# Second attention of a three-layer transformer kernel: scores from stacked parts, packed values, transfers on SyncE's queue

## The chip, the cores and the metric

The kernel runs as one program on one core of a Trainium2 chip. The metric is the device time of one execution in microseconds; lower is better. TensorE multiplies, VectorE (DVE) and ScalarE (ACT) work element by element, GpSimd (POOL) makes the low parts of weights, SyncE (SP) issues transfers.

## The reference, cut to what matters

A block of two layers is followed by a third of another kind, on 512 positions of width 1024. Layer 0 has differential attention, layer 1 (the "second attention" here) windowed attention with grouped keys, layer 2 forgetting attention beside a convolution. All arithmetic is float32. The second attention, cut down:

```
q, k, v = split(h @ w_qkv)           # 16 query heads, 4 key/value heads, head dim 64
q, k = rope(q), rope(k)
s = einsum(q, k) * 64**-0.5          # only |i-j| <= 128: blocks of 128, at most 3 key blocks
m = max(max(s), sink)                # one sink logit per head
e = exp(s - m)
pr = e / (sum(e) + exp(sink - m))
o = einsum(pr, v) @ w_o
```

h is the RMS-normed residual; the result is added to the residual.

## The kernel before, in words

**Float32 by two parts.** Each operand is split into a high part (dtype fp32r, the rounded value) and a low part (value minus high part). `mm3` makes a product of three matmuls: high x high, high x low, low x high. The product low x low is left out. ScalarE makes high parts, VectorE low parts; for weights GpSimd makes the low part.

**Weights.** They come as slabs of 128 x 1024 (512 KB). SyncE's `load` issues one transfer per slab, in order, into one of two raw buffers (`RAWS = 2`); load s waits until GpSimd has made the low part of slab s-2 (`lo_ready`). ScalarE's `high` makes the high part into a ring of four (`RING = 4`) when TensorE is done with the slab four earlier (`used`, `replaced`). All that is a fixed order on each engine: nothing overtakes. SyncE's queue holds the slab loads of the whole kernel and, in the first attention, small `exchange` transfers between partitions.

**The second attention** (kind 2). Stage `kq2a` has two slabs: the first pair of key heads and the first pair of query heads (tile j holds two heads). `v2` has two slabs for the values, and `kq2` eight slabs: the second pair of key heads, then the query tiles 1 to 7. After a tile is projected, ScalarE's `swap_halves` (L1187) makes four copies of 32x512 out of PSUM, VectorE's `rope` (L1716, L1717, L1720) rotates, `q_high` (ScalarE, L1193) and `q_low` (VectorE, L1743) make the parts in `qkhi`, `qklo`, indexed [partition, buffer, query or key, position]; a pair of heads takes partitions 0-63 and 64-127. TensorE's `project_qk` can do a part of a tile; `open_tile` waits until the PSUM bank is free, which `rope`'s first product releases (L1716). All tiles of `kq2` but the first use one bank, that of the last value tile too, which `values_low` (L1693) releases.

The values are written with zeros beside them (`padded`): the head u of a pair has its 64 columns at 64u of a 128-column block, high parts in `Bhi[1]`, low parts in `Blo[1]`. `zero_padding("v2")` clears the rest with four memsets. So both heads of a pair add into one PSUM tile of 128 rows (bank 7).

**Steps.** There are 8 pairs of heads j and 4 query blocks qb, in all 32 steps g = 4j + qb, and in each two heads s. In step g TensorE issues: `scores(g + 2)`, a quarter of a projection (`piece` says which; with g % 4 == 0 it comes last, `late`), `transposes(g)`, and in even steps `outputs(g - 1)`, for two query blocks. Projections end with step 23. `scores` (L708) makes for each of two heads an `mm3` on 64 partitions (columns: 256 or 384 keys), then masks by a product with the identity, once with the high constants and once with their copy in the other half of the partitions: ten matmuls a step, three of products and two of masks for each head. `outputs` (L777) makes 18 matmuls: 3 spans of keys x 2 heads x 3.

VectorE per step: `maxima(g + 2)` (L1753 to L1768), `rope` or `q_low` where a tile is due, `normalise(g + 1)` (L1782 to L1797), `prob_low(g)` (L1805). ScalarE per step: `exps(g + 1)` (L1207, L1216), `prob_high(g)` (L1228), `q_high`, every fourth step `evacuate` (L1235, a copy of 128x512 of bank 7 into `OA`), `swap_halves`, `replaced`. In the last steps `output_high` and `output_low` split `OA` for the output projection `o2`.

**Start.** TensorE: both tiles of `kq2a`, the values, `scores(2, 0)`, tile 0 of `kq2` (second keys), tile 1, `scores(2, 1)`, then the steps. ScalarE's order there: swaps, high parts of slabs 0 and 1 of `kq2`, `q_high`, high parts of slabs 2 and 3 of `kq2` (after the value slabs are used), then the high parts of the values.

## Time and profile before

| | us |
|---|---|
| median of 3 runs | 2091.57 |
| lowest, highest | 2088.61, 2092.48 |
| span of the profiled execution | 2087.8 |

The page gives no time of the profiled execution beyond its span. The span lies 3.8 us under the median of the runs. In it TensorE is busy 2043.2 us, VectorE 1224.2, ScalarE 941.6, GpSimd 904.8. The second attention's steps run from about 741 to 888 us.

How to read the rows. A timeline has the start in us, the length in us, the engine, the line in the kernel, the operation, out<-in by the program's names, the shapes and a count; in brackets the idle time before and what ended it. PE is TensorE's matmul, PEld its weight load, SPq SyncE's queue. Matmul ends are modelled, so rates are taken from start to start. A group adds the busy time (overlaps counted once) and the mean ns of one. In a table of stretches each engine has its busy us and its instructions; then come the granted clock of TensorE (1.00 is full), the busy share of the 16 DMA engines and the GB/s moved. A waits row says who waited for whom, us in total, times, the longest.

### The profile page before, as it was taken

How to read it: one execution, taken by the hardware profiler on the slowest of the kernel's cores; microseconds unless marked ns; L12 is line 12 of the kernel's file. 1: busy time of each engine (PE TensorE's matmuls, PEld its weight loads, DVE VectorE, ACT ScalarE, POOL GpSimd, SP SyncE). 2: the span in 40 equal slices, each digit the busy share in tenths (PEclk: the TensorE clock that was granted, in tenths of full speed). 3: DMA queues.
4: the chain of work that ended last, by engine and by line, in shares of the span. 5: the costliest groups of instructions: out<-in, count | busy, mean ns of one | idle time of the engine just before them, and what ended most of it. 6: DMA issues, size and time to landing. Idle time of an engine off the chain costs nothing.

```text
span 2087.8 us, 28730 instructions
## 1 busy us (share of the span) xinstructions
PE 2043.2 (98%) x9976; PEld 1684.1 (81%) x9976; DVE 1224.2 (59%) x1842; ACT 941.6 (45%) x1495; POOL 904.8 (43%) x660
## 2 busy tenths in 40 slices
PE   7999999999999999899999999999999999999999
PEld 6777788888887878788888887878888788888887
DVE  6677857546265789856636266548879473213222
ACT  5456645434245567635424245535742544322222
POOL 4322235545456431044645456444215454455454
PEclk9999999999999999999999999999999999999999
DMA  4222122332323211022333223222103222232323
GB/s 169 81 76 76 48 75 98 103 101 91 101 91 121 81 61 32 31 91 81 101 101 101 92 99 112 91 81 92 39 23 107 85 91 92 90 110 92 101 91 111
DMA packets 52756, 183.21 MB, mean 88 GB/s; under 512 B 6576, under 2 KB 6832, under 8 KB 52656
## 3 DMA queue, kind: packets, MB, share of 16 engines
q1 hardware_dynamic: 51072, 177.76, 25.9%
q10 hardware_dynamic: 1584, 4.07, 0.5%
q8 instruction: 68, 1.11, 0.2%
q14 instruction: 32, 0.26, 0.0%
HBM read 176.04 MB, written 2.10 MB: 85 GB/s over the span
## 4 chain that ended last, share of the span: by engine, by line
PE 53%; issue 24%; POOL 13%; DVE 7%; ACT 2%; POOLq 0%; DVEq 0%; DMA 0%; ACTq 0%; SPq 0%
PE PS L544 52%; POOL wlo L536 13%; DVE AR L1915 1%; PE PS L773 1%; DVE AR L1918 0%; DVE acc L1630 0%; DVE ptlo L1805 0%; DVE AR L1797 0%; DVE nmax L1753 0%; ACT AR L1187 0%; DVE AR L2277 0%; ACT AR L1323 0%; DVE AR L1931 0%; DVE Blo L1935 0%; DVE Blo L2281 0%
## 5 line engine op out<-in xcount | busy, mean ns | idle before, releaser
L536 POOL TENSOR_TENSOR wlo<-raw,whi 128x512 fp32r<-128x512 f32 x656 | 904.6, 1402 | 1169.7 <-ACT whi L1090 1168.5
L544 PE MATMUL PS<-Bhi,whi 128*128 128x512 f32 x2352 | 927.7, 394 | 17.2 <-DVE Blo L1623 10.8
L544 PE MATMUL PS<-Blo,whi 128*128 128x512 f32 x2352 | 917.6, 390 | 0.0
L544 PE MATMUL PS<-Bhi,wlo 128*128 128x512 f32 x2352 | 917.4, 390 | 0.0
L1090 ACT ACTIVATE whi<-raw 128x1024 fp32r<-128x1024 f32 x328 | 345.2, 1056 | 510.7 <-PE PS L544 435.4
L544 PEld LDWEIGHTS PS<-Bhi,whi 128*128 128x128 f32 x2352 | 442.5, 188 | 123.1 <-issue 14.1
L544 PEld LDWEIGHTS PS<-Bhi,wlo 128*128 128x128 f32 x2352 | 442.6, 188 | 93.7
L544 PEld LDWEIGHTS PS<-Blo,whi 128*128 128x128 f32 x2352 | 443.0, 188 | 89.3 <-issue 0.5
L1614 DVE TENSOR_TENSOR AR<-PS,R 128x512 f32<-128x512 f32 x170 | 115.3, 690 | 235.9 <-PE PS L544 224.1
L1670 DVE TENSOR_TENSOR X<-X,PS 128x512 f32<-128x512 f32 x88 | 60.3, 687 | 227.2 <-PE PS L544 226.5
L1915 DVE SCALAR_TENSOR_TENSOR AR<-AR,par_sb 128x511 f32<-128x511 f32 x88 | 117.6, 1336 | 8.8 <-ACT AR L1323 8.8
L1338 ACT ACTIVATE Bhi<-AR 128x512 f32 x66 | 41.8, 633 | 167.7 <-DVE AR L1931 167.7
L1918 DVE SCALAR_TENSOR_TENSOR AR<-AR,par_sb 128x511 f32<-128x511 f32 x88 | 106.8, 1213 | 12.9 <-DVE AR L1915 2.9
L1207 ACT ACTIVATE AR<-PS,nmax 128x512 f32<-128x512 f32 (+3 forms) x160 | 93.2, 590 | 44.1 <-DVE nmax L1756 41.7
L1323 ACT ACTIVATE AR<-AR,par_sb 128x512 f32<-128x512 f32 x88 | 71.0, 806 | 38.5 <-DVE AR L1614 38.5
L1935 DVE TENSOR_TENSOR Blo<-AR,Bhi 128x512 f32 x66 | 47.1, 714 | 62.1 <-ACT Bhi L1338 62.1
L1623 DVE SCALAR_TENSOR_TENSOR Blo<-X,par_sb,Bhi 128x512 fp32r<-128x512 f32 x56 | 63.0, 1135 | 34.9 <-ACT Bhi L1116 27.7
L1228 ACT ACTIVATE pthi<-PS 128x512 fp32r<-128x512 f32 (+3 forms) x128 | 56.4, 477 | 59.1 <-PE PS L773 58.4
L1931 DVE TENSOR_TENSOR AR<-AR 128x512 f32<-128x512 f32 x66 | 56.1, 849 | 36.3 <-ACT AR L1334 27.2
L1630 DVE TENSOR_TENSOR acc<-acc,sq 128x512 f32<-128x512 f32 x56 | 73.2, 1308 | 0.0
L773 PE MATMUL PS<-constR,AR 128*128 128x128 f32 x368 | 58.3, 286 | 10.6 <-DVE ptlo L1805 9.7
L1805 DVE TENSOR_TENSOR ptlo<-PS,pthi 128x512 fp32r<-128x512 f32 (+3 forms) x128 | 64.3, 534 | 6.7 <-ACT pthi L1228 6.7
(237 smaller groups left out, 2069.1 us busy)
## 6 DMA issues: line engine op xcount, KB each, us to landing
raw<-in_weights SPq DMA_DIRECT2D x328, 512.0 KB, 3.2
AR<-AR SPq DMA_DIRECT2D x56, 64.0 KB, 2.0
X<-in_xT ACTq DMA_DIRECT2D x4, 512.0 KB, 6.9
out<-X SPq DMA_DIRECT2D x8, 256.0 KB, 3.0
AR<-in_pT ACTq DMA_DIRECT2D x2, 512.0 KB, 3.9
par_sb<-in_parameters ACTq DMA_DIRECT2D x1, 314.0 KB, 8.5
AR<-in_positions ACTq DMA_DIRECT2D x1, 256.0 KB, 8.3
con_sb<-in_constants ACTq DMA_DIRECT2D x1, 198.5 KB, 8.1
```

The costliest lines, as they stand in the source:

```text
L536: ins = pool.tensor_tensor(wlo[:, j, c], raw[:, j % RAWS, c], f32(whi[:, j, c]), ALU.subtract)
L544: return pe.matmul(out, w, x, start=start, stop=stop)
L773: last = pe.transpose(PS[:, 2 + n % 2, k * P:k * P + P], source[:, k * P:k * P + P], ident)
L1090: act.activation(whi[:, slot, :], raw[:, slot % RAWS, :], ACT.Copy)\
L1207: act.activation(probs(kind)[:, 2 * (g % 2) + s, 0:nb * P], PS[:, score_bank(kind, n), 0:nb * P], ACT.Exp, bias=nmax[:, n % 4:n % 4 + 1], ...
L1323: act.activation(cv[:, 2 * pair + u, :], us[:, 2 * pair + u, :], ACT.Identity, scale=conv_w[:, l, 1, u, bass.ds(q, 1)], bias=conv_w[:, l, ...
L1614: tt(out, PS[:, bank, :], R[:, :], ALU.mult).then_inc(tile_free[bank], 1)
L1623: stt(chunks(Blo[b])[:, m, :], X[:, m, :], gain(name, col, m), f32(chunks(Bhi[b])[:, m, :]), ALU.mult, ALU.subtract).then_inc(x_split, 1)
L1630: tt(acc[:, :], acc[:, :], sq[:, slot, :], ALU.add).then_inc(sq_used, 1)
L1805: tt(transposed(ptlo, kind, g, s), PS[:, 2 + n % 2, 0:blocks * P] .rearrange("p (k q) -> p k q", k=blocks), f32(transposed(pthi, kind, g, s)),
L1915: own.step(stt(c[:, 1:T], x[:, 0:T - 1], conv_w[:, l, 0, u, bass.ds(q, 1)], c[:, 1:T], ALU.mult, ALU.add))
L1918: stt(c[:, 0:T - 1], x[:, 1:T], conv_w[:, l, 2, u, bass.ds(q, 1)], c[:, 0:T - 1], ALU.mult, ALU.add).then_inc(conv_done, 1)
```

## The change

Scores: `qkhi` and `qklo` become two halves of one tile `qk`. SyncE gets two new jobs. `stack_keys(kb)` makes four transfers of 256 KB that write the high and the low key parts of each head of pair kb into both halves of the partitions (`stackk`, in `Blo[1]`). `stack_queries(j)` makes four transfers of 128 KB that put a head's high query part into one half of the partitions and its low part into the other (`stackq`, in the end of `Bhi[1]`, two buffers). They wait for `q_ready`, and stand in SyncE's order ahead of the loads `of_k + 6`, `of_q + 6` and `of_q + j + 6`. With `of_q = of_k + 4`, the first keys and queries stand ahead of the load of slab 2 of `kq2`. TensorE's scores wait for the transfers and make per head two matmuls of 128 rows (the product low x low comes with them) and one mask.

Values: `padded(..., low=True)` writes the low part of a head into the other 64 columns of its block in `Bhi[1]`. `outputs` then makes two matmuls per span and head, 12 in all, and the two heads go to two halves of bank 7; the part from the low values lies in the other half of the partitions. `evacuate_part` (ScalarE, two copies of 64x256 across the halves) and `add_parts` (VectorE, two additions of 64x256) follow every second step; `outputs` waits for the last `add_parts`. `zero_padding("v2")` is gone.

Projections: `piece` is one step further on in kind 2 (a tile ends with g % 4 == 2), `late` is g % 4 == 3, and at g == 0 two quarters are made at the end of the step.

```diff
@@ -200,8 +200,8 @@
         Bhi = [sb(f"Bhi{n}", [P, KC * T], F32R) for n in range(2)]
         Blo = [sb(f"Blo{n}", [P, KC * T], F32R) for n in range(2)]
-        qkhi = sb("qkhi", [P, 2, 2, T], F32R)
-        qklo = sb("qklo", [P, 2, 2, T], F32R)
+        qk = sb("qk", [P, 2, 2, 2, T], F32R)
+        qkhi, qklo = qk[:, 0], qk[:, 1]
         pthi = sb("pthi", [P, 6, T], F32R)
         ptlo = sb("ptlo", [P, 6, T], F32R)
         R = sb("R", [P, T])
@@ -290,6 +290,11 @@
         cvo = ar(7296, 4)
         frow = AR[0:8, 3072:3072 + 3 * T].rearrange("p (n t) -> p n t", n=3)
         angs = ar(5120, 6)
+        stackq = Bhi[1][:, TB * T:].rearrange("p (b s t) -> p b s t", b=2, s=2)
+        stackk = Blo[1][:, :].rearrange("p (h l t) -> p h l t", h=4, l=2)
         raw_ready = [sem(f"raw_ready{n}") for n in range(RAWS)]
...
@@ -362,7 +370,7 @@
         PAIRS = {1: 8, 2: 8, 3: 4}
-        def padded(stage, B, src, t):
+        def padded(stage, B, src, t, low=False):
@@ -370,7 +378,8 @@
             v = B[1][:, 0:TB * nh * P].rearrange("p (k n c) -> p k n c", k=TB, n=nh)[:, t]
             v = v.rearrange("p (n two) c -> p n two c", two=2)
             s = src.rearrange("p (n two c) -> p n two c", two=2, c=64)
-            return [(v[:, :, u, 64 * u:64 * u + 64], s[:, :, u, :]) for u in range(2)]
+            at = [64 * u if not low else 64 - 64 * u for u in range(2)]
+            return [(v[:, :, u, at[u]:at[u] + 64], s[:, :, u, :]) for u in range(2)]
         def band(kind, qb):
@@ -388,7 +397,7 @@
         PB0 = {1: 0, 2: 32, 3: 96}
         GROUP = 2
         PV0 = {1: 0, 2: 16, 3: 32}
-        OP0 = {1: 0, 2: 8, 3: 16}
+        OP0 = {1: 0, 2: 8, 3: 24}
         QT0 = {1: 0, 2: 16, 3: 26}
@@ -398,7 +407,7 @@
-            first = 7 if kind == 1 else 8
+            first = {1: 7, 2: 9, 3: 8}[kind]
             p, r = (g + first) // 4, (g + first) % 4
             t, part, parts = {1: (2 * p - 2 + r // 2, r % 2, 2), 2: (p, r, 4),
                               3: (2 * p + r // 2, r % 2, 2)}[kind]
@@ -515,7 +524,45 @@
                 if first <= s < first + NPROJ[1]:
                     exchange(s - first + 2)
                 load(s, s % RAWS, s - 1)
-            with sp.Fori((first + NPROJ[1] + 3) // 4, SLABS // 4) as i:
+            def stack_keys(kb):
+                n = QT0[2] + 2 * kb
+                sp.wait_ge(q_ready, n + 1)
+                for s in range(2):
+                    rows = slice(64 * s, 64 * s + 64)
+                    for to in range(0, P, 64):
+                        sp.dma_start(f32(stackk[to:to + 64, 2 * kb + s, :, :]), f32(qk[rows, :, kb, 1, :]))\
+                            .then_inc(kstacked[kb], 16)
+            def stack_queries(j):
+                b = j % 2
+                sp.wait_ge(q_ready, QT0[2] + (1 if j == 0 else j + 2) + 1)
+                if j >= 2:
+                    sp.wait_ge(score_done, SC0[2] + 8 * (j - 1))
+                for s in range(2):
+                    rows = slice(64 * s, 64 * s + 64)
+                    for half in range(2):
+                        to = 64 * (half ^ s)
+                        sp.dma_start(f32(stackq[to:to + 64, b, s, :]), f32(qk[rows, half, b, 0, :]))\
+                            .then_inc(qstacked[b], 16)
+            begin, of_k, of_q = SLAB0["kq2a"] // 4 * 4, SLAB0["kq2a"], SLAB0["kq2"]
+            end = -(-(of_q + NPROJ[2] + 6) // 4) * 4
+            stacks = {of_k + 6: ((stack_keys, 0), (stack_queries, 0)), of_q + 6: ((stack_keys, 1),)}
+            for j in range(1, 8):
+                stacks[of_q + j + 6] = ((stack_queries, j),)
+            with sp.Fori((first + NPROJ[1] + 3) // 4, begin // 4) as i:
+                for j in range(4):
+                    load(4 * i + j, j % RAWS, 4 * i + j - 1)
+            for s in range(begin, end):
+                for stack, n in stacks.get(s, ()):
+                    stack(n)
+                load(s, s % RAWS, s - 1)
+            with sp.Fori(end // 4, SLABS // 4) as i:
                 for j in range(4):
                     load(4 * i + j, j % RAWS, 4 * i + j - 1)
             for m in range(KC):
@@ -710,14 +757,17 @@
                 b = j % 2
                 kb = j // 4 if kind == 2 else b
                 first, nb, masks = band(kind, qb)
-                if g == 0 and kind > 1:
+                if g == 0 and kind == 3:
                     pe.wait_ge(swapped_ready, 2)
                 if g == {2: 1, 3: 0}.get(kind):
                     all_values(kind)
-                if qb == 0:
-                    pe.wait_ge(q_ready, QT0[kind] + {1: 2 * j + 2, 2: 2 if j == 0 else j + 3,
-                                                     3: 2 * j + 2}[kind])
+                if qb == 0 and kind == 2:
+                    pe.wait_ge(qstacked[b], 64 * (j // 2 + 1))
+                    if j % 4 == 0:
+                        pe.wait_ge(kstacked[kb], 64)
+                elif qb == 0:
+                    pe.wait_ge(q_ready, QT0[kind] + 2 * j + 2)
                     if kind == 3 and j == 0:
                         pe.wait_ge(cc_ready, 1)
@@ -735,12 +785,21 @@
                     rows, cols = slice(64 * s, 64 * s + 64), slice(qb * P, qb * P + P)
                     keys = slice(first * P, (first + nb) * P)
                     out = PS[:, score_bank(kind, n), 0:nb * P]
+                    if kind == 2:
+                        for half in range(2):
+                            mm(out, stackq[:, b, s, cols], stackk[:, 2 * kb + s, half, keys],
+                               half == 0, False)
+                        blocks = out.rearrange("p (b c) -> p b c", c=P)
+                        at, c = [block for block, _ in masks], masks[0][1]
+                        mm(blocks[:, at[0]:at[-1] + 1:2, :], constR[:, 0, :], constR[:, c:c + len(masks), :],
+                           False, True).then_inc(score_done, 1)
+                        continue
                     last = mm3(out, qkhi[rows, b, 0, cols], qklo[rows, b, 0, cols],
                                qkhi[rows, kb, 1, keys], qklo[rows, kb, 1, keys], True, kind == 1)
                     if kind == 1:
                         last.then_inc(score_done, 1)
                     outs.append(out)
-                if kind == 1:
+                if kind < 3:
                     return
                 for s, out in enumerate(outs):
                     rows = slice(64 * s, 64 * s + 64)
@@ -780,7 +839,10 @@
                 heads = HP[kind]
                 pe.wait_ge(pt_ready, PB0[kind] + heads * (g + 1))
-                if last_qb == GROUP - 1 and OP0[kind] + j:
+                if kind == 2:
+                    pe.wait_ge(o_ready, OP0[2] + g // GROUP)
+                elif last_qb == GROUP - 1 and OP0[kind] + j:
                     pe.wait_ge(o_ready, OP0[kind] + j)
                 nh = {1: 8, 2: 4, 3: 8}[kind]
@@ -794,6 +856,18 @@
                     if qs:
                         spans.append((len(qs) == 2, k, qs[0], qs[-1] + 1))
                 spans.sort(reverse=True)
+                if kind == 2:
+                    for s in range(2):
+                        head = 2 * (j // 4) + s
+                        for n, (_, k, a, b) in enumerate(spans):
+                            r, c = row_of(kind, g, s, k), (a - q0) * P
+                            out = PS[:, 7, 2 * P * s + c:2 * P * s + (b - q0) * P]
+                            for half, buf in enumerate((pthi, ptlo)):
+                                last = mm(out, vhi[:, k, head, :], keys_of(buf, kind, g)[:, r, c:c + (b - a) * P],
+                                          n == 0 and half == 0, n == len(spans) - 1 and half == 1)
+                    last.then_inc(pv_done, 1)
+                    return
                 work = [(k, a, b, 0) for _, k, a, b in spans]
                 if kind != 1:
@@ -865,7 +939,7 @@
                 for g in range(steps):
                     if g + AHEAD[kind] < steps:
                         scores(kind, g + AHEAD[kind])
-                    late = kind == 2 and g % 4 == 0
+                    late = kind == 2 and (g % 4 == 3 or g == 0)
                     if piece(kind, g) and not late:
                         t, part, parts = piece(kind, g)
                         project_qk(PROJ[kind], norm, t - 2 if kind == 3 else t, part, parts)
@@ -889,6 +963,8 @@
                         half_tile("o1a", 0, range(4))
                     if piece(kind, g) and late:
                         t, part, parts = piece(kind, g)
+                        if g == 0:
+                            project_qk(PROJ[kind], norm, t, 0, parts)
                         project_qk(PROJ[kind], norm, t, part, parts)
                     if kind == 1 and g in SPREAD:
                         spread_factor(SPREAD[g])
...
@@ -1234,6 +1310,14 @@
                 act.wait_ge(pv_done, PV0[kind] + (j + 1) * (4 // GROUP))
                 act.activation((OA3 if kind == 3 else OA)[:, j, :], PS[:, 7, :], ACT.Copy)\
                    .then_inc(o_ready, 1)
+            def evacuate_part(e):
+                act.wait_ge(pv_done, PV0[2] + e + 1)
+                j, c = e // 2, slice(2 * P * (e % 2), 2 * P * (e % 2) + 2 * P)
+                act.activation(OA[0:64, j, c], PS[64:128, 7, 0:2 * P], ACT.Copy)
+                act.activation(OA[64:128, j, c], PS[0:64, 7, 2 * P:4 * P], ACT.Copy).then_inc(part_ready, 1)
             def output_square(h):
@@ -1275,7 +1359,9 @@
                         for c in OSPLIT.get(g, ()):
                             output_high(OA, c)
-                    if g % 4 == 0 and g:
+                    if kind == 2 and g % GROUP == 0 and g:
+                        evacuate_part(g // GROUP - 1)
+                    if kind != 2 and g % 4 == 0 and g:
                         evacuate(kind, g // 4 - 1)
                         if kind == 1:
                             output_square(g // 4 - 1)
...
@@ -1685,7 +1774,7 @@
                                  for b in (Blo[1], Bhi[1])]
                             parts = [(v[0], PS[:, bank, :], v[1])]
                         else:
-                            lo = padded(stage, Blo, PS[:, bank, 0:width], t)
+                            lo = padded(stage, Bhi if stage == "v2" else Blo, PS[:, bank, 0:width], t, stage == "v2")
                             hi = padded(stage, Bhi, PS[:, bank, 0:width], t)
                             parts = [(a, s, b) for (a, s), (b, _) in zip(lo, hi)]
                         for q, (out, src, hi) in enumerate(parts):
@@ -1838,10 +1927,21 @@
                 bank, _ = tile_of(stage, 0, m)
                 tt(X[:, m, :], X[:, m, :], PS[:, bank, :], ALU.add).then_inc(tile_free[bank], 1)
+            def add_parts(e):
+                j, c = e // 2, slice(2 * P * (e % 2), 2 * P * (e % 2) + 2 * P)
+                dve.wait_ge(part_ready, e + 1)
+                for s in range(2):
+                    rows = slice(64 * s, 64 * s + 64)
+                    ins = tt(OA[rows, j, c], OA[rows, j, c], PS[rows, 7, 2 * P * s:2 * P * s + 2 * P], ALU.add)
+                    if s == 0:
+                        own.step(ins)
+                ins.then_inc(o_ready, 1)
             def output_low(src, c):
                 hi, lo = ((pthi[:, c, :], ptlo[:, c, :]) if src is OA3 else
                           (chunks(Bhi[0])[:, c, :], chunks(Blo[0])[:, c, :]))
-                dve.wait_ge(ohi_ready, OP0[3 if src is OA3 else 2] + c + 1)
+                dve.wait_ge(ohi_ready, (16 if src is OA3 else 8) + c + 1)
                 tt(lo, src[:, c, :], f32(hi), ALU.subtract).then_inc(o_split, 1)
             def attention(kind):
@@ -1892,8 +1992,12 @@
                         if g in OTILE:
                             add_half("o1a", OTILE[g])
                     if kind == 2:
+                        if g and g % GROUP == 0:
+                            add_parts(g // GROUP - 1)
                         for c in OSPLIT.get(g, ()):
                             output_low(OA, c)
+                if kind == 2:
+                    add_parts(steps // GROUP - 1)
             def feed_forward(l):
                 factor(f"ffn{l}")
...
```

## Rows read from the trace of the kernel before

**Rows 1.** The page, part 1: busy us (share of the span) xinstructions, by engine.
```profile
PE 2043.2 (98%) x9976; PEld 1684.1 (81%) x9976; DVE 1224.2 (59%) x1842; ACT 941.6 (45%) x1495; POOL 904.8 (43%) x660
```

**Rows 2.** Table of stretches, second attention: PE, PEld, DVE, ACT, POOL busy, clock, DMA, GB/s.
```profile
780.90:797.50 16.60, 16.44 (x120) 13.76 (x120) 15.07 (x45) 11.96 (x36) 2.54 (x2) 1.00 0.10 34
...
863.80:876.20 12.40, 10.74 (x80) 9.71 (x80) 10.63 (x34) 6.77 (x23) 2.51 (x2) 0.83 0.14 45
876.20:888.10 11.90, 7.74 (x64) 6.68 (x64) 10.27 (x27) 8.74 (x24) 0.00 (x0) 1.00 0.00 1
```

**Rows 3.** Waits, 764.4 to 863.8 us: who for whom, total, times, longest.
```profile
DVE AR L1716 <- ACT AR L1187: 2.2, 5, 0.5
...
DVE nmax L1753 <- PE PS L544: 0.8, 4, 0.2
```

**Rows 4.** Groups by shape, 740 to 887 us: busy us, mean ns, idle before.
```profile
L544 PE MATMUL PS<-qkhi 64*128 64x384 f32 x32 | 7.1, 432 | 0.0
```

**Rows 5.** TensorE's timeline (start, us, what): outputs, scores of 256 and of 384.
```profile
790.46 0.36 PE L544 MATMUL PS<-pthi,Bhi 128*128 128x256 f32 x1
...
792.52 0.28 PE L544 MATMUL PS<-pthi,Blo 128*128 128x256 f32 x1
...
797.51 0.39 PE L544 MATMUL PS<-qkhi 64*128 64x256 f32 x2
...
798.24 0.50 PE L544 MATMUL PS<-Bhi,whi 128*128 128x512 f32 x1
...
869.48 0.45 PE L544 MATMUL PS<-qkhi 64*128 64x384 f32 x2
...
870.45 0.66 PE L773 MATMUL PS<-constR,AR 128*128 128x128 f32 x4
```

**Rows 6.** Timelines of VectorE and ScalarE, 789 to 790 us.
```profile
789.40 0.75 DVE L1805 TENSOR_TENSOR ptlo<-PS,pthi 128x256 fp32r<-128x256 f32 x2
790.06 1.01 DVE L1753 TENSOR_REDUCE nmax<-PS 128x1 f32<-128x384 f32 x2
...
789.57 2.39 ACT L1187 ACTIVATE AR<-PS 32x512 f32<-32x512 f32 x4
```

**Rows 7.** Transfers: SP's timeline, two stretches of the table, issues with landing time.
```profile
93.08 2.41 SPq L510 DMA_DIRECT2D AR<-AR  x4
...
94.20:96.60 2.40, 2.40 (x13) 1.73 (x12) 2.33 (x5) 1.42 (x5) 2.32 (x2) 1.00 0.45 109
97.50:99.20 1.70, 1.70 (x11) 1.37 (x10) 1.67 (x4) 0.51 (x1) 0.00 (x0) 1.00 0.94 294
...
AR<-AR SPq DMA_DIRECT2D x56, 64.0 KB, 2.0
```

**Rows 8.** Timelines of all engines, 733 to 748 us, ahead of the first scores.
```profile
733.63 6.40 POOL L536 TENSOR_TENSOR wlo<-raw,whi 128x512 fp32r<-128x512 f32 x4 [10.25 <-ACT whi L1090]
...
737.10 3.48 DVE L1743 SCALAR_TENSOR_TENSOR qklo<-AR,qkhi 128x512 fp32r<-128x512 f32 x2
...
740.69 0.39 PE L544 MATMUL PS<-qkhi 64*128 64x256 f32 x2
...
747.73 0.47 PE L544 MATMUL PS<-Bhi,whi 128*128 128x512 f32 x1 [0.54 <-DVE Blo L1693]
...
743.68 1.06 ACT L1090 ACTIVATE whi<-raw 128x1024 fp32r<-128x1024 f32 x1 [1.45 <-DMA raw<-in_weights]
```

**Rows 9.** Timelines, 759 to 767 us, ahead of the second pair's scores.
```profile
759.21 0.69 DVE L1743 SCALAR_TENSOR_TENSOR qklo<-AR,qkhi 128x512 fp32r<-128x512 f32 x1
...
763.63 0.68 DVE L1743 SCALAR_TENSOR_TENSOR qklo<-AR,qkhi 128x512 fp32r<-128x512 f32 x1
...
766.21 0.75 DVE L1753 TENSOR_REDUCE nmax<-PS 128x1 f32<-128x256 f32 x2
...
760.98 2.52 POOL L536 TENSOR_TENSOR wlo<-raw,whi 128x512 fp32r<-128x512 f32 x2 [13.61 <-ACT whi L1090]
...
764.37 0.39 PE L544 MATMUL PS<-qkhi 64*128 64x256 f32 x2 [0.17 <-DVE qklo L1743]
```

15 lines of the change are left out of this document (10 added, 5 removed).

## The prediction

> **What bounds the kernel now.** I read the page's busy times first, then the second attention by itself: a table of stretches, the matmuls of it grouped by shape, its waits, and the timelines of single steps. TensorE is busy 98% of the span [rows 1], so a shorter TensorE stage looks like a shorter kernel. The stage says otherwise. A pair of heads (four steps) repeats every 16.6 us, and in it TensorE is busy 16.44 us but VectorE also 15.07 us (the first row of [rows 2]). In the last eight steps, which have no projection beside them, VectorE is busy 10.63 of 12.4 and 10.27 of 11.9 us, TensorE no longer ahead in the last stretch (second and third row). So VectorE stands just behind TensorE in six pairs and ahead of it in the last two: what TensorE loses there, only a VectorE that has room can turn into time. In 99.4 us of steady state VectorE waits for ScalarE's swaps 2.2 us and for scores 0.8 us [rows 3], 0.5 us a pair; the rest of its idle time lies between dependent little operations and stays.
>
> **Scores.** Before, each (step, head) has three products on 64 rows and two masks on 64 rows; the two heads stand in different halves of the array. The rows show that they run at once: 32 matmuls of 64x384 of 432 ns mean would be 13.8 us, and are 7.1 us busy [rows 4]. A step's ten matmuls thus cost five passes. After, two products of 128 rows per head and one mask each: six matmuls, six passes, four of them wide. From the first score matmul to the next instruction, five passes take 0.97 us with 384 columns and 0.73 us with 256 (the two pairs of score rows in [rows 5]). A 256-column pass takes 2.18/18 = 0.12 us (a group of output matmuls, from 790.46 to 792.52 + 0.12, counts the 128-column ones as nearly as long); a 384-column pass about 0.17. After: 4x0.17 + 2x0.12 = 0.92, and 4x0.12 + 2x0.11 = 0.70. Saved on TensorE: 16x0.05 + 16x0.03 = 1.3 us, not the two fifths that the instruction count suggests. Bounds: -3 us (a loss, if the changeover between 64 and 128 rows was already hidden) to +4 us (if it costs 0.1 us at each end now).
>
> **Outputs.** Each group of two steps has 18 matmuls and 2.18 us; after, 12: 1.45 us. TensorE saves 0.73 us x 16 groups = 11.6 us, for certain. With the scores TensorE has 13 us less to do, about 1.5 us per pair.
>
> **What pays for it on VectorE and ScalarE.** The two halves of the accumulator must now be added: per group ScalarE makes two copies of 64x256 out of PSUM and VectorE two additions of 64x256, instead of one 128x512 copy every second group. No such addition is in the trace; the nearest row is a subtraction from PSUM of 128x256, two in 0.66 us from start to start of what follows [rows 6]. Bounds 0.4 us (half the partitions cost less) to 1.4 us (each waits for its part). I take 0.66: 1.33 us per pair. VectorE then has 15.07 + 1.33 = 16.4 us of work alone. The period if all that VectorE waits now vanished: 16.57 - 0.5 + 1.33 = 17.4 us, +0.8 a pair. Bounds: 16.4 (-0.2) and 18.6 (+2). Six pairs (764 to 864) make +5 us, bounds -1 and +12. The four ACT swaps (2.39 us [rows 6]) now come a step earlier, behind the evacuation and ahead of the next exponentials; ScalarE has idle time there (it waits for transposes), so I price that at nothing; if its cover is gone, exps come late and the upper bound holds. In the last eight steps four groups' additions count, 4x0.66 = 2.6 us, against 3.4 us of VectorE's idle there: I take +2, bounds 0 and +4. The last group's is hidden by the output projection's first seven chunks.
>
> **Transfers, first place.** Before the first scores, SP must move the doubled keys (four transfers of 256 KB) and the stacked queries (four of 128 KB), SBUF to SBUF. Nearest: the exchanges, 64 KB each, four issues in 2.41 us, 2.0 us to landing, and 109 GB/s at a DMA share of 0.45 over their stretch, that is 242 GB/s at full share; slabs 294/0.94 = 313 GB/s [rows 7]. The low parts of key and query take 3.48 us for both, so they end at 738.8 and 740.6 [rows 8]. Keys issued 738.8 to 741.3, queries to 743.7; data starts 1.2 us after an issue: keys until 740.1 + 4.3 = 744.4, queries until 746.6, landed about 747. The first scores start at 740.69 now: TensorE stands 6.3 us. Worse, the loads of two slabs are behind these in SP's queue and in the DMA queue. Now the second of them is issued when GpSimd ends (740.03) and ScalarE gets it at 743.68 [rows 8], 3.65 us, of which 1.2 before data and 1.7 data. After, both slabs' data run from 746.6 to 750.0 and land at about 750.8: 7.1 us later. Behind that wait on ScalarE stand the v2 high parts, then VectorE's low parts, and those release the projection at 747.73 [rows 8]. The 6.3 us and the 7.1 us run beside each other: +7. Bounds +3 (transfers twice as quick, and the slabs before them) and +11 (rate halved).
> SBUF — State Buffer, "Door 1: The DMA port swizzle" in the Trainium skill, says that a transfer over 64 partitions covers only half of the ports, measured 196 GB/s at 1 MiB. At that rate each 1.57 MB would take 8.0 us, not 6.5, and with the second place below the sum would be 3 us longer.
>
> **Second place.** Keys of the second half go out when their low part is done (before: 759.21 + 0.69, now +7: 766.9): 4.3 us of data from 768.1 to 772.4. Next in SP's queue is a slab load that waits for GpSimd (ends 763.5 [rows 9], +7 = 770.5): data to 774.1. Only then the queries of pair 1, ready at 763.63 + 0.68, +7 = 771.3: data to 776.3, landed 776.8. Without the transfers TensorE would start those scores at 764.37 + 7 = 771.4, with no slack now (they start as the low part ends). 5.4 us late, less 1.1 us that VectorE takes before it wants them (maxima at 766.21, last score in at about 765.1) [rows 9]: +4, bounds +1 and +7. In later pairs the projection is one step sooner, the low part ends some 3 us before the place where scores start at the earliest, and VectorE wants them 2 us later: four issues and a landing (2.4 + 2.0) fit just about; within the bound of +2 a pair.
> The deleted zeroing of four 128x512 blocks gives nothing: TensorE works through the projection's last chunk in that time.
>
> **Sum.** +7 + 4 + 5 + 2 = +18 us. TensorE's 13 us are not in it: they lie beside VectorE's work and in its own new waits. The bounds add up to +3 and +34. The profiled span is 2087.8 us, the median of the runs 2091.6, 3.8 us (0.2%) above; that lies around the span and stays: 2109.6, I say 2109.5 us.
>
> **Rivals.**
> 1. Faster, 2085: TensorE alone sets the period, as its 16.44 busy of 16.6 says, VectorE takes the additions in its 1.5 us of idle time per pair, and stacks land quickly: -13 + 4 + 2 = -7. It decides if a pair's period falls under 15.6 us. Against: 15.07 + 1.33 alone is above 16 us. Chance 0.15.
> 2. Break even, about 2092: half of TensorE's saving comes through and pays for the first transfers. Period about 16 us. 0.11.
> 3. Much slower, 2126: each group closes a loop: outputs, copies on ScalarE, additions on VectorE, while exps of the next step stand behind the copies and the swaps. If each of 16 groups holds VectorE for another microsecond: +16. For: SP's and ScalarE's orders are fixed and each wait holds what is behind. Against: outputs are 0.73 us shorter. TensorE's granted clock would fall more often: it is 0.83 in the stretch with TensorE busy 10.74 of 12.4 us (the second row of [rows 2]). 0.14.
> 4. The forecast, its own range 2098 to 2121: 0.60.
>
> The time should lie between 2088 and 2124: above, it takes in most of rival 3; below, half of rival 2 and the foot of rival 1. About 0.2% (4 us) is what a measurement can tell from no change. Faster by more than that: 0.15. Within: 0.07 of rival 2. Slower: 0.60 + 0.14 + 0.04 = 0.78.
>
> **What would show it.** Score matmuls at 128 rows, x192, with no two at once; outputs 12 per group; TensorE idle some 6 us before the first scores, released by a DMA, ScalarE waiting for a slab to about 750, and a second stop of about 4 us some 30 us later. A pair's period of 17.4 us with VectorE busy over 95% of it. I am wrong if the period is below 16.57 us, if TensorE isn't stopped at the first scores, or if the slabs land before the stacks.

## The result, and the profile after

The changed kernel takes 2123.1 us (median of 4 runs, 2122.7 to 2123.8), the kernel before 2090.1 us (4 runs, 2084.0 to 2092.5): a ratio of 1.0164, interval 1.015 to 1.0179. The forecast was +18 us; it came to +33 us. The direction was right, the size not: it lies above the forecast's own 2098 to 2121 us. It is just inside the outer range of 2088 to 2124 us, which went above 2121 only to take in most of the "much slower" rival (2126 us).

Page, part 1 of the changed kernel, beside [rows 1]:

```profile
PE 2039.0 (96%) x9752; PEld 1686.0 (79%) x9752; DVE 1239.8 (58%) x1870; ACT 950.0 (45%) x1519; POOL 902.7 (43%) x660
```

TensorE has 224 matmuls less and is busy 4 us less, in a span 33 us longer; the half-clock stretches below give back most of what it saved. Its waits in the whole second attention (735 to 920 us; columns: engine and line, whom it waits for, total, times, longest):

```profile
PE PS L591 <- DMA Bhi<-qk: 16.8, 5, 8.1
PE PS L591 <- DVE AR L1805: 14.7, 6, 2.7
PE PS L832 <- DVE ptlo L1894: 13.0, 10, 3.0
```

Three waits share the loss: for the stacked queries (transfers), for VectorE's rope before the late quarter of the projection, and of the transposes for VectorE. Between 764.4 and 863.8 us, the stretch of [rows 3], TensorE had none of the first two before, and of the third only this:

```profile
PE PS L773 <- DVE ptlo L1805: 1.5, 1, 1.5
```

**Where the stage starts.** The profiled executions do not reach this stage at the same time. VectorE's low parts of the first keys and queries, behind which the new transfers go out, start at 737.10 us before [rows 8] and here at 734.55; kernels 7 and 8 below differ only in the steps behind them and start them at 737.72 and 733.93. So places are compared by their distance from that row. First the changed kernel's two rows (low parts, first maxima), then the first maxima before:

```profile
734.55 3.48 DVE L1832 SCALAR_TENSOR_TENSOR qk<-AR,qk 128x512 fp32r<-128x512 f32 x2
...
752.18 0.74 DVE L1842 TENSOR_REDUCE nmax<-PS 128x1 f32<-128x256 f32 x2
```

```profile
747.50 0.75 DVE L1753 TENSOR_REDUCE nmax<-PS 128x1 f32<-128x256 f32 x2
```

The distance is 10.4 us before and 17.6 us after: +7.2 us.

**The two stops.** SP's queue and TensorE at the first and at the second place (start, us, what, idle before):

```profile
736.36 3.39 SPq L536 DMA_DIRECT2D Blo<-qk  x4
...
745.20 0.79 PE L591 MATMUL PS<-Blo,Bhi 128*128 128x256 f32 x2 [7.03 <-DMA Bhi<-qk]
...
747.07 1.06 ACT L1166 ACTIVATE whi<-raw 128x1024 fp32r<-128x1024 f32 x1 [11.78 <-DMA raw<-in_weights]
...
764.80 3.33 SPq L536 DMA_DIRECT2D Blo<-qk  x4
...
769.29 3.04 SPq L550 DMA_DIRECT2D Bhi<-qk  x4
...
776.81 0.80 PE L591 MATMUL PS<-Blo,Bhi 128*128 128x256 f32 x2 [8.11 <-DMA Bhi<-qk]
...
797.07 0.50 PE L591 MATMUL PS<-Blo,Bhi 128*128 128x256 f32 x2 [0.40 <-DMA Bhi<-qk]
```

Both stops are where they were expected. From the third pair on the transfer is late three times, by 0.40 us (last row), 0.73 and 0.57 us. The table of the changed kernel (as [rows 7]) tells the rate, and that the clock is low in the stretches with these stops:

```profile
738.00:744.50 6.50, 0.16 (x2) 0.00 (x0) 0.03 (x1) 0.00 (x0) 0.00 (x0) 0.82 0.95 228
...
760.00:780.00 20.00, 10.02 (x50) 8.39 (x49) 12.45 (x36) 9.40 (x26) 5.03 (x4) 0.82 0.53 132
...
800.00:820.00 20.00, 16.28 (x93) 14.02 (x94) 17.55 (x49) 13.01 (x38) 2.53 (x2) 0.91 0.21 56
...
840.00:860.00 20.00, 16.40 (x108) 14.11 (x108) 18.74 (x56) 13.97 (x40) 2.51 (x2) 1.00 0.25 70
```

**A steady pair.** I measure pairs from the first of VectorE's maxima of one pair of heads to that of the next. Before: 18.7, then 16.6 six times. After: 25.6, 22.5, 19.9, 19.9, 18.3, 19.9, 18.7. So the first pair takes 6.9 us more and the next six together 19.8 us more. With the 7.2 us ahead of them and 1.8 us behind the last of these maxima, less the 2.55 us by which this execution was ahead at the low parts, that is the 33.1 us between the two spans. First TensorE's timeline in a pair of the changed kernel, as in [rows 5]:

```profile
792.28 0.36 PE L591 MATMUL PS<-pthi,Bhi 128*128 128x256 f32 x1
...
793.71 0.45 PE L591 MATMUL PS<-Blo,Bhi 128*128 128x256 f32 x2
...
794.41 0.45 PE L591 MATMUL PS<-Bhi,whi 128*128 128x512 f32 x1
...
802.21 0.56 PE L591 MATMUL PS<-Blo,Bhi 128*128 128x384 f32 x2
...
803.21 0.70 PE L832 MATMUL PS<-constR,AR 128*128 128x128 f32 x4
806.47 0.47 PE L591 MATMUL PS<-Bhi,whi 128*128 128x512 f32 x1 [2.56 <-DVE AR L1805]
...
808.66 0.84 PE L591 MATMUL PS<-Blo,Bhi 128*128 128x384 f32 x2
...
810.37 0.44 PE L591 MATMUL PS<-Bhi,whi 128*128 128x512 f32 x1
```

ScalarE's timeline beside it, the copies (L1320), the swaps (L1263) and the exponentials (L1283):

```profile
802.81 0.38 ACT L1320 ACTIVATE AR<-PS 64x256 f32<-64x256 f32 x1
803.21 2.39 ACT L1263 ACTIVATE AR<-PS 32x512 f32<-32x512 f32 x4
805.62 0.47 ACT L1283 ACTIVATE AR<-PS,nmax 128x256 f32<-128x256 f32 x1
```

And VectorE's: a group's additions (L1936), maxima, and the rope's addition out of PSUM (L1805):

```profile
803.26 0.86 DVE L1936 TENSOR_TENSOR AR<-AR,PS 64x256 f32<-64x256 f32 x2
804.15 1.02 DVE L1842 TENSOR_REDUCE nmax<-PS 128x1 f32<-128x384 f32 x2
...
805.63 0.69 DVE L1805 TENSOR_TENSOR AR<-PS,AR 128x512 f32<-128x512 f32 x1
```

Outputs: 792.28 to 793.71, 1.43 us. Scores of 256: 0.70 us, of 384: 1.00 us. At 803.2 TensorE issues its transposes and stands: the late quarter may write its bank only when the rope's addition (805.63) has read it, and that waits for the four swaps on ScalarE (to 805.60), which stand behind the two copies of the output. TensorE waits 2.56 us, and then its granted clock is at the lower level: the scores of 384 at 808.66 take 1.71 us, not 1.00. There are six such waits (1.87 to 2.67 us). After three of them the clock fell (before 806.47, 826.35 and 864.53), after three it did not. The pair from 840 on has one of the latter: it takes 18.3 us where the pairs with the fallen clock take 19.9, though TensorE stands there just as long (2.55 us before 846.24). So the low clock alone costs 1.6 us a pair.

### The profile page after: what moved, and what is told of

It reads as the page before. It is cut to its first block, busy times and chain, and to the rows that moved or that the text cites. A ratio compares the mean times of both kernels' runs of the same rounds, so it can differ in the third digit from the quotient of the medians.

```text
span 2120.9 us, 28334 instructions
## 1 busy us (share of the span) xinstructions
PE 2039.0 (96%) x9752; PEld 1686.0 (79%) x9752; DVE 1239.8 (58%) x1870; ACT 950.0 (45%) x1519; POOL 902.7 (43%) x660
## 4 chain that ended last, share of the span: by engine, by line
PE 55%; issue 24%; POOL 14%; DVE 4%; ACT 2%; POOLq 0%; DMA 0%; SPq 0%; DVEq 0%; ACTq 0%
PE PS L591 55%; POOL wlo L583 14%; PE PS L832 1%; ACT AR L1263 1%; DVE acc L1719 0%; DVE AR L1886 0%; DVE ptlo L1894 0%; DVE AR L1936 0%; DVE nmax L1842 0%; DVE AR L2380 0%; DVE Blo L2384 0%; ACT Bhi L1192 0%; DVE X L1759 0%; DMA Bhi<-qk 0%; DVE nmax L1853 0%
## 5 line engine op out<-in xcount | busy, mean ns | idle before, releaser
L591 PE MATMUL PS<-Bhi,whi 128*128 128x512 f32 x2352 | 927.6, 394 | 28.6 <-DVE AR L1805 14.7
L1283 ACT ACTIVATE AR<-PS,nmax 128x512 f32<-128x512 f32 (+3 forms) x160 | 93.0, 587 | 43.3 <-DVE nmax L1845 40.6
L832 PE MATMUL PS<-constR,AR 128*128 128x128 f32 x368 | 59.8, 290 | 17.6 <-DVE ptlo L1894 16.8
L832 PEld LDWEIGHTS PS<-constR,AR 128*128 128x128 f32 x368 | 46.0, 149 | 30.4 <-DVE AR L1886 16.2
```

What stands on the lines that cost most here:

```text
L591: return pe.matmul(out, w, x, start=start, stop=stop)
L832: last = pe.transpose(PS[:, 2 + n % 2, k * P:k * P + P], source[:, k * P:k * P + P], ident)
L1283: act.activation(probs(kind)[:, 2 * (g % 2) + s, 0:nb * P], PS[:, score_bank(kind, n), 0:nb * P], ACT.Exp, bias=nmax[:, n % 4:n % 4 + 1], ...
```

## Experiments

Each ratio is against the unchanged kernel before, run beside it (2089 to 2091 us), and each interval is 95%. "Kernel 2" is the kernel of experiment 2, and so on.

**1. Projections back.** The changed kernel with the projections where they stood before:

```
-            first = {1: 7, 2: 9, 3: 8}[kind]
+            first = 7 if kind == 1 else 8
...
```

(`late` is g % 4 == 0 again with it.)

> The changed kernel with one part undone: the quarters of the projections stand again where they stood before (a tile ends with step g % 4 == 3, the late quarter comes at the end of a step with g % 4 == 0). Loop theory (the late quarter in step 3 waits 2.56 us for its bank behind ScalarE's swaps and keeps the next scores from VectorE): that idle time goes, but the stacked queries are issued one step later and TensorE waits for them in each pair some 3 us, so the time moves little, 2115 to 2125. Rival, additions theory (the pair's 19.9 us come from VectorE's additions and ScalarE's copies alone): no change from the idle going, and the same new wait: about 2130. Third: the step sooner does no harm and its loss costs the full 3.8 us of transfers in 7 pairs: 2145.

2147.6 us, 1.0281 [1.0262, 1.0300], nearest to the third answer. From the second on pairs take 22.5 to 24.0 us, as each waits for its queries (waits, 735 to 925 us):

```profile
PE PS L591 <- DMA Bhi<-qk: 47.7, 8, 8.2
```

The step sooner is no ornament: without it the transfer stands bare in every pair, 5.3 to 5.7 us from the third on.

**2. Sooner alone.** The kernel before with only that step (the diff above reversed, and its `late` rule).

> The kernel before with one part of the change alone: projections one step sooner. Loop theory: also here TensorE stands some 2 us at the late quarter in step 3 in each of six pairs, and the pair grows from 16.57 to 17.5 to 18.5 us: 2096 to 2102. Additions theory: no additions here, so no change: 2088 to 2092.

2107.3 us, 1.0086 [1.0062, 1.0110]: +17 us with nothing else changed, 5 us above the range that I gave. Pairs of 18.8 to 20.4 us; TensorE stands 1.71 us before the late quarter, and in the third to fifth pair it runs at the lower clock behind it (its timeline):

```profile
813.25 0.47 PE L544 MATMUL PS<-Bhi,whi 128*128 128x512 f32 x1 [1.71 <-DVE AR L1718]
...
815.64 0.69 PE L544 MATMUL PS<-qkhi 64*128 64x384 f32 x2
```

**3. Packed values alone.** The kernel before with the packed values, the copies and additions of halves, without zeroing; no stacks, nothing sooner.

> The packed values alone, with their copies and additions: scores as before (three products on 64 rows), no stacked transfers, projections where they stood before. VectorE theory: 12 instead of 18 output matmuls give nothing, the additions cost 1.78 us of VectorE a pair: the pair goes from 16.57 to 17.5 to 18.2 us, and the time is 2097 to 2104. Rival, TensorE sets the period: 11.6 us less matmul time show and the time is 2080 to 2086.

2096.8 us, 1.0035 [1.0022, 1.0047]: +7 us, which is what the forecast had for the additions (+5 and +2). But it doesn't come evenly: pairs take 18.7, 18.8, 16.5, 18.2, 16.5, 17.1 and 19.1 us, so a pair can hold its 16.5 us with the additions in it. The loss is in single pairs and the tail, where the table shows a granted clock of 0.75 over 40 us:

```profile
860.00:900.00 40.00, 26.08 (x152) 22.88 (x152) 32.84 (x90) 24.11 (x72) 2.61 (x2) 0.75 0.05 14
```

**4. Small additions.** The changed kernel with additions of 2 columns instead of 256.

```
-  ins = tt(OA[rows, j, c], OA[rows, j, c], PS[rows, 7, 2*P*s:2*P*s + 2*P], ALU.add)
+  ins = tt(OA[rows, j, d], OA[rows, j, d], PS[rows, 7, 2*P*s:2*P*s + 2], ALU.add)
```

> The changed kernel, VectorE's additions of the two halves cut from 64x256 to 64x2 (the output lacks most of the low parts' product). Additions theory: VectorE gets 1.6 us of 19.9 back in each pair and 0.7 us in each group of the last eight steps, in all 11 to 14 us: 2110. Loop theory: in the six pairs VectorE only waits longer at the next scores, under 1 us a pair comes back, in all 3 to 7 us: 2117 to 2120.

2123.4 us, 1.0163 [1.0144, 1.0181]: nothing, where both answers had something back. The length of each group's additions (0.89 us) is not what a pair lasts for. The copies and the additions' places in the order stay in this kernel, so it says nothing of them. TensorE's waits before the late quarter stay too (2.7 us the longest).

**5. Outputs a step later (kernel 2 with them).** Outputs and their copy come one step later, so that they again lie between step 3's scores and the late quarter's wait:

```
-                    if g and g % GROUP == 0:
+                    if kind != 2 and g and g % GROUP == 0:
                         outputs(kind, g - 1)
+                    if kind == 2 and g > 2 and g % GROUP:
+                        outputs(kind, g - 2)
```

> The kernel before, projections one step sooner as in e6 (2107), and the output matmuls of two steps one step later, ahead of the late quarter of step 3 (ScalarE's evacuation moved with them). Cover theory: in e6 TensorE stands 1.7 us at the late quarter because 2.2 us of output matmuls now lie ahead of the scores of step 3 and no longer between the swaps and the quarter; the idle time also halves the granted clock for some 3 us in each pair. Put back as cover they end both: the pair falls from 19.9 to 16.6 to 17.6 us, clock 1.00, and the time is 2090 to 2097. Rival, order on ScalarE: the swaps ahead of the exponentials of the next pair make the loss wherever the outputs stand: 2104 or more.

2094.9 us (12 runs), 1.0026 [1.0016, 1.0035]: 12.4 of the 17 us are back. The third to sixth pair take 16.5 us again; the first, second and last do not (19.6, 19.1, 19.8). The table of 785 to 865 us, first of kernel 2:

```profile
785.00:865.00 80.00, 72.00 (x485) 58.46 (x483) 65.17 (x180) 48.27 (x143) 10.15 (x8) 0.94 0.08 27
```

and the same stretch of this kernel:

```profile
785.00:865.00 80.00, 74.40 (x549) 62.08 (x548) 73.00 (x210) 57.95 (x170) 12.73 (x10) 0.98 0.09 30
```

In the same 80 us TensorE gets 549 matmuls done, not 485, its clock is 0.98, not 0.94, and VectorE is busy 73.0 us, not 65.2. Kernel 2 waits 6.8 us for the rope there (four times), this one not at all. So most of the cost of "sooner" is that the output matmuls no longer cover the wait for the rope.

**6. The same in the changed kernel.**

> The changed kernel with the outputs, copies and additions one step later, as in e10. Cover theory: pairs 2 to 6 fall from 19.9 (18.3 at full clock) towards 17 to 18 us, the first two stops for stacked operands stay: 2108 to 2114. Rival, order on ScalarE: 2120 to 2124.

2126.1 us, 1.0175 [1.0154, 1.0196]: a miss; nothing came back. The wait for the rope is gone (12.9 to 2.7 us between 785 and 865 us), but the transposes wait 12.3 us there for `prob_low`, which stands behind a normalising of 2.73 us (0.75 where nothing is beside it). GpSimd's splitting of a slab runs then (its timeline, VectorE's, and the waits of 785 to 865 us):

```profile
812.50 2.61 POOL L583 TENSOR_TENSOR wlo<-raw,whi 128x512 fp32r<-128x512 f32 x2 [16.96 <-ACT whi L1168]
```

```profile
812.60 2.73 DVE L1888 TENSOR_SCALAR AR<-AR,rinv 128x384 f32<-128x384 f32 x2
```

```profile
PE PS L832 <- DVE ptlo L1896: 12.3, 6, 2.7
```

**7. The changed kernel without stacks** (scores as before; packed values and sooner stay).

> The changed kernel without the stacks: scores as before from the split queries and keys, no transfer of queries or keys; packed values, copies and additions, and the projection one step sooner stay. Each of the two alone cost 6.8 and 17 us. If the parts add up and the transfers and stacked scores carry the rest, this runs at 2090 + 24 = 2114 us, its steady pairs take 19.9 us, and TensorE waits for no transfer. If the loss of the packed values and that of the sooner projection are the same idle time, told twice (both sit between the additions and the next exponentials), it is nearer 2107 to 2109 and the transfers with the stacked scores cost 15 us. If the shorter output groups make the missing cover worse than in the kernel before, it is above 2117.

2110.4 us, 1.0101 [1.0072, 1.0131]: +19.3, less than 17 + 7, between the two first answers. The stacks cost the other 13.7 us. By pairs this kernel has 19.6, 21.4, 18.5, 20.1, 20.0, 20.1, 18.7, and its first maxima come 10.1 us after the start of the low parts (737.72 to 747.86); in the changed kernel it is 17.6. So the stacks cost 7.5 us at the first place, 5.9 and 1.1 in the first two pairs, and in the next five pairs together -0.7 us (96.6 against 97.4): 13.8 us.

**8. That kernel with the outputs a step later.**

> The kernel above (no stacks, packed values, sooner) with the output matmuls, the copies out of PSUM and the additions one step later, as was done to the changed kernel without any gain and to the kernel with the sooner projection alone with 12 of 17 us back. If the packed values with their copies and additions are what eats the gain (VectorE's normalising meets GpSimd's work, the transposes wait 2.7 us a pair), this too stays within 3 us of the kernel above, with a pair at 18.9 us or more. If the stacked scores and their transfers ate it, this kernel gets 10 us or more back, to 2104 us or less, with pairs near 16.6 us.

2101.3 us, 1.0059 [1.0040, 1.0078]: 9 us back, the third to sixth pair take 17.6 us. That is nearer to the second answer: with outputs a step later the stacks cost 24.8 us (2126.1 against 2101.3), not 13.7, and the same move brings nothing where they are. Its normalising meets GpSimd too, but starts 0.16 us ahead of it and takes 1.77 us:

```profile
811.79 1.77 DVE L1876 TENSOR_SCALAR AR<-AR,rinv 128x384 f32<-128x384 f32 x2
```

**9. Kernel 6 with the slab's split first.** ScalarE's high part of the slab, which releases GpSimd, goes ahead of the exponentials of its step:

```
                     begun, halfway = finished(kind, g - 1), finished(kind, g - 2)
+                    if kind == 2 and halfway is not None:
+                        replaced("kq2", halfway)
                     if g + 1 < steps:
                         exps(kind, g + 1)
```

> The changed kernel with outputs, copies and additions a step later (19.0 us a pair, 2126 us), and in it ScalarE's high part of the freed slab, which starts GpSimd's 2.6 us of splitting, moved ahead of the exponentials of the same step instead of behind the transposed probabilities, some 2 us sooner. If the collision of GpSimd's splitting with VectorE's normalising (two 128x384 in 2.73 us, 0.75 where nothing is beside them) is what eats the gain, normalising takes under 1.5 us, TensorE's 2.7 us wait per pair shrinks, pairs take 17.5 us or less, and the time is 2126 - 6 x 1.5 = 2117 us or less. If the loss is a chain that closes anyway (the copies, the transfers, the scores), something else is stretched in its place, or the exponentials are late by the 1 us of the slab's high part, and it stays at 2123 to 2130 us.

2121.9 us, 1.0162 [1.0141, 1.0183]. The third to sixth pair take 18.05 us (19.2 on average in kernel 6), normalising is at 0.75 us, and the clock is 1.00 between 785 and 865 us (0.94 in kernel 6): the collision was a cause of kernel 6's loss, worth 1.1 us a pair. Not of all of it: what GpSimd meets now is a little subtraction of 128x2, 0.16 us alone, and the first pair went from 25.6 to 28.2 us. There the slab's high part (1.06 us) stands ahead of the exponentials, and the second keys are issued at 768.23 us, in kernel 6 at 765.57 (the two executions start the first low parts within 0.05 us of each other). The total misses the 2117 us by both: four steady pairs gave 4.5 us together, where I had 9 us in six, and the first took 2.6 back. GpSimd's and VectorE's timelines:

```profile
811.27 2.53 POOL L583 TENSOR_TENSOR wlo<-raw,whi 128x512 fp32r<-128x512 f32 x2 [15.53 <-ACT whi L1168]
```

```profile
812.60 1.21 DVE L1859 TENSOR_TENSOR sdiff<-nmax,nsink 128x2 f32<-128x2 f32 x1
...
814.72 0.75 DVE L1888 TENSOR_SCALAR AR<-AR,rinv 128x384 f32<-128x384 f32 x2
```

**10. Order of the transfers.** Slabs ahead of the first stacks (a), and pair 1's queries ahead of the second keys (b):

```
-  stacks = {of_k + 6: ((stack_keys, 0), (stack_queries, 0)), of_q + 6: ((stack_keys, 1),)}
(a) stacks = {of_q + 4: ((stack_keys, 0), (stack_queries, 0)), of_q + 6: ((stack_keys, 1),)}
(b) stacks = {of_k + 6: (...same...), of_q + 6: ((stack_queries, 1),), of_q + 7: ((stack_keys, 1),)}
```

> The changed kernel, the first stacked keys and queries moved behind the loads of slabs 2 and 3 of kq2. My step said that the stop at the first scores and the late slabs run beside each other. If the slabs are what counts (values' high parts, then the bank): the time falls by 5 to 7 us, 2116 to 2118. If TensorE's own stop for the stacked operands counts (its two projections stand behind it): ScalarE no longer waits for slabs until 747 us, but the steps start hardly sooner, -2 to +1 us: 2121 to 2124.

> The changed kernel, the queries of pair 1 ahead of the second half's keys and ahead of one slab load in SyncE's order; the keys one load later. Queue theory: TensorE's second stop (8.1 us, until 776.8) is made of keys and a slab ahead of the queries in the queue; it shrinks by 3.5 to 5 us and so does the time: 2118 to 2120. Rival: the stop comes from four issues and a landing alone, and the time does not move.

(a) 2127.3 us, 1.0181 [1.0164, 1.0198]: 4 us worse than the changed kernel and than both answers, TensorE's longest stop 10.6 us. (b) 2121.5 us, 1.0151 [1.0134, 1.0168]: the second stop is 4.75 us, not 8.11, and the first pair takes 22.3 us, not 25.6:

```profile
776.45 0.79 PE L591 MATMUL PS<-Blo,Bhi 128*128 128x256 f32 x2 [4.75 <-DMA Bhi<-qk]
```

From the low parts (737.43 here) to the last pair's maxima this execution is 3.2 us shorter than the changed kernel's, so the stop is taken away and not moved: keys and a slab ahead of the queries were part of it, as the queue theory says. The medians differ by 1.7 us only, and the runs overlap (2120.1 to 2124.1 against 2122.7 to 2123.8), so at the end the gain is not clear of the noise.

**11. Stale queries.** Kernel 1 with queries stacked for pairs 0 and 1 only; the other pairs use those, and no transfer is waited for.

> Stacked scores without their transfers in steady state: as e1 (projections where they stood before, 2148), but queries are stacked for pairs 0 and 1 only, and later pairs use those again (the scores of pairs 2 to 7 are of the wrong queries). Pass theory (six passes cost what five cost with two heads at once): pairs 2 to 6 take what they take with packed values alone, 16.5 to 18.2 us, and only the two first stops remain: 2108 to 2114. Rival (fewer matmuls are less time): pairs under 16 us, 2100 to 2105. If six passes cost more: 18.5 us and over, 2118 or more.

2117.0 us, 1.0135 [1.0115, 1.0156], 3 us above the pass theory's range, though nearly all steady pairs are in its range. The third to seventh pair take 18.0 us on average (17.56 three times), not less than kernel 3's 17.5: two products of 128 rows for three of 64 rows, two heads at once, save nothing that reaches the time, even with the transfers free.

**12. Two quarters at once.** The late quarter of step 3 goes to the end of step 0, with the next one, so that nothing waits on the swaps' rope in step 3.

> The changed kernel, the quarter at the end of steps 3 (mod 4) moved to the end of the following step, where now two quarters stand one behind the other; nothing else. Loop theory: TensorE's 2.56 us of idle time before that quarter goes, scores reach VectorE sooner, the granted clock stays at 1.00 in steady state, and the pair falls from 19.9 to about 18 us: 2108 to 2112. Additions theory: VectorE's work is the same, the pair stays at 19.5 or more: 2121 to 2124.

2132.6 us, 1.0206 [1.0187, 1.0225]: 9.5 us slower than the changed kernel, above both answers. TensorE now waits for exponentials, which free the scores' bank and stand behind the swaps on ScalarE, and its clock over 785 to 865 us is 0.83 (waits of that stretch):

```profile
PE PS L591 <- ACT AR L1282: 9.7, 4, 2.4
```

With both orders of 10 and a later `scores(2, 0)` besides, it was 2125.4 us, 1.0171 [1.0154, 1.0188], above both answers again.

> The changed kernel with four changes of order: first stacks behind two slab loads, queries of pair 1 ahead of the second keys, both quarters at the end of the step with g % 4 == 0, and the first kq2 projection ahead of the first scores. If the three stops found are the loss: 33 us shrink by 5 to 7 (first stop, hidden by the projection), 4 (second) and 10 to 12 (steady state), leaving the additions: 2100 to 2105. If VectorE's additions are most of it: 2112 or more.

Kernel 5 is the best of the variants with "sooner", and the kernel before is 0.26% ahead of it; none of the versions tried beats the kernel before.

## Why the prediction was right or wrong

- **What bounds the kernel.** Right: TensorE's 13 us less bought nothing. In the 20 us with the clock at 1.00 (840 to 860) VectorE is busy 18.74 us, 94%, and TensorE 16.40. In the 20 us before them it is busy 17.5, 88%, where my sign was over 95% and a pair of 17.4 us: VectorE's work bounds a pair from below, and did not set it.
- **Scores.** 1.00 us (384) against 0.92, 0.70 (256) against 0.70; with 0.97 and 0.73 before, nothing saved instead of 1.3 us. Six passes for five, as argued; kernel 11 shows that it is worth nothing.
- **Outputs.** 12 matmuls in 1.43 us; forecast 1.45.
- **Additions.** 0.89 us a group from start to start, forecast 0.66, in the bounds; but kernel 4 shows that their length is not on the path of a pair. My reason for +0.8 a pair (VectorE's sum of work) was not what decided it.
- **The step that failed: "The four ACT swaps now come a step earlier ... so I price that at nothing", and with it the period of 17.4 us.** I had looked at ScalarE's room and not at what TensorE does meanwhile. Before, the output matmuls stand between the last scores ahead of the rope and the late quarter that waits for it; a step sooner they are already done. TensorE stands 1.7 us (kernel 2) or 2.56 us (all changes), in half of the pairs its clock is low for some 3 us behind that, and exponentials stand behind the swaps. The forecast had +5 us for the six pairs behind the first; they took 19.8 more. In kernel 2, which has nothing but the step sooner, they took 18.3 more, and the changed kernel's six waits for the rope are 14.7 us. Kernel 2 prices the step at 17 us, kernel 5 takes 12.4 of them back by putting the cover back. The bound that I gave for "if its cover is gone" (18.6 us a pair) had no term for the clock: the pair without the low clock (18.3 us) lies inside it, those with it (19.9 us) outside.
- **Transfers, first place.** Right. Forecast +7 with TensorE stopped 6.3 us and both slabs in at about 750.8, which is 748.3 in an execution that is 2.55 us ahead. It stopped 7.03 us; ScalarE had the slabs at 747.07 and 748.37. Counted from the low parts the first maxima came 7.2 us later than before, 7.5 later than without stacks. The rate was right: 228 GB/s at a DMA share of 0.95 is 240 at full share, against the 242 from [rows 7]. The Trainium skill's 196 GB/s for 64 partitions (SBUF — State Buffer, "Door 1: The DMA port swizzle") did not show here, where transfers from and into both halves run side by side.
- **Second place.** Forecast +4, a stop of about 4 us: TensorE stood 8.11 us, and the first pair lost 5.9 us to the stacks (kernel 7 against the changed kernel), in the bounds of 1 to 7. I had keys, slab and queries in the queue, 2.1 MB. The next slab came in beside the queries (issued 772.82): 2.62 MB moved from 764 to 778 us, and the queries took 4.7 us from issue to landing, 2.3 in later pairs. Issuing took longer as well, 3.3 and 3.0 us for four each, not 2.4. Kernel 10 (b) shows that the order ahead of the queries is worth 3.4 us of the stop; the share of the other two is not shown.
- **Later pairs' transfers "fit just about".** Right: 0.40 to 0.73 us late at three, and kernel 1 shows 5.3 to 5.7 us bare without the step sooner. So the first place and the first two pairs (7.5, 5.9, 1.1) are all that the stacks cost, where the forecast had 11.
- **Zeroing.** Right: no gain shows. From the norm's last low part to the low parts of keys and queries it is 13.13 us with it (723.97 to 737.10, before) and without it (721.42 to 734.55, after).
- **Rivals.** The faster two needed a period under 16 us; it never was. "Much slower" named 16 groups that each hold VectorE 1 us; the time came near its time, and a falling clock was named in it. Its price, the microsecond of VectorE per group, is not what happened: kernel 4 takes the additions' length away and nothing comes back. "Exps behind the copies and the swaps" was right as to place. What the copies ahead of the swaps cost by themselves no kernel tells.
- **Luck.** That the time is inside the outer range is luck: the size of the steady pairs was wrong, and the range reached to 2124 for a rival with another price.

The 33 us, by differences of medians: packed values 6.8; sooner, on top of these, 12.5 (17 when alone); stacks 13.7, nearly all at two places. The parts overlap, so other orders of taking them give other shares.

**Open.** Kernel 9 has the stacks, little wait for the rope (2.6 us in five, 785 to 865 us) and a clock of 1.00, and its pairs still take 18.05 us, where kernel 8 takes 17.6 with a collision. What the last half microsecond is (GpSimd's new place, or the scores, one pair of 384 columns 1.00 us long) no run tells apart. Why packed values alone lose in single pairs and the tail I know only as far as the low clock beside it.

## What to carry to other kernels

When work moves a step earlier, look not only at whether its own engine has room, but at what lay between its waits on the engine that waits for it: cover that moves to the wrong side of a wait costs the wait, and the matmuls behind it at the lower clock. Count passes and not matmuls where two tiles of the array run at once, before paying with transfers for fewer of them. A remedy for one wait has to be tried in the kernel in which it is wanted: the same move gave 12 us in one, 9 in the next and none in the third, in part as it put a VectorE operation beside GpSimd's. And executions are to be lined up at a common row just ahead of the stage before its places are compared: here they come to it up to 4 us apart.

## What was unexpected of the hardware

- A stop of 2.56 us in a stretch where TensorE is otherwise busy was followed by matmuls at 1.2 GHz for about 3 us (starts 0.43 us apart from 807.4 to 808.7, where 0.23 is usual); that cost 1.6 us a pair beside the stop itself. Of six such stops (1.87 to 2.67 us) three were followed by it; in kernel 2 stops of 1.71 us were too.
- Normalising two 128x384 blocks (SBUF to SBUF) takes 0.75 us alone, 1.77 us if it starts just ahead of GpSimd's pair of 128x512 subtractions (1.27 us each), and 2.73 us if just behind. A subtraction of 128x2 took 1.21 us, not 0.16, beside it; the maxima of 128x384 out of PSUM at 811.04 in kernel 9 started 0.23 us before GpSimd and kept their 1.02 us. The Trainium skill (SBUF — State Buffer, "Who interferes with whom") says that the port pair which the two engines share is locked for a whole instruction, by whichever starts first, and that a reduction never contends; the traces agree.
- SP takes 2.4 us to issue four transfers of 128 KB between partitions when its queue is clear, 3.0 to 3.6 us behind others, and 3.3 to 3.4 us for four of 256 KB.
